# Convolution two, split over three engines, and a second paired chunk in a two-layer decoder trunk on one Trainium2 core

## The reference

```python
def odd_layer(x, g_norm, w_pw1, w_dw, b_dw, g_conv, w_pw2):
    h = rms_norm(x, g_norm)
    z = h @ w_pw1
    y = z[..., :D_MODEL] * jax.nn.sigmoid(z[..., D_MODEL:])
    y = lax.conv_general_dilated(
        y, w_dw[:, None, :].astype(y.dtype), window_strides=(1,),
        padding=[(CONV_WIDTH - 1, 0)], dimension_numbers=('NWC', 'WIO', 'NWC'),
        feature_group_count=D_MODEL) + b_dw            # CONV_WIDTH = 31, each channel by itself
    y = jax.nn.silu(rms_norm(y, g_conv))
    return x + y @ w_pw2

def channel_mixer(x, g_norm, w1, w2):
    h = rms_norm(x, g_norm)
    return x + jnp.square(jax.nn.relu(h @ w1)) @ w2
```

## Time and profile before

| | us |
|---|---|
| median of 3 runs | 2148.29 (2146.34 to 2148.51) |
| the profiled execution | 2146.37 |
| its span, first to last instruction | 2144.6 |
| TensorE busy | 2108.4 |
| GpSimd busy | 1075.8 |
| VectorE busy | 1368.5 |

### The profile page before, as it was taken

How to read it: one execution, slowest core, us unless ns; L and a number is a source line. 1 busy time by engine, 2 the same in 40 slices (tenths; PEclk the granted TensorE clock), 3 DMA queues, 4 the chain that set the end, 5 groups by cost and what they waited for, 6 DMA issues and landing times.

```text
span 2144.6 us, 30725 instructions
## 1 busy us (share of the span) xinstructions
PE 2108.4 (98%) x9946; PEld 1761.0 (82%) x9946; DVE 1368.5 (64%) x2158; ACT 876.7 (41%) x1320; POOL 1075.8 (50%) x652
## 2 busy tenths in 40 slices
PE   7999899999999999999999999999999999999999
PEld 6887788888888998888888888788888888888887
DVE  6697758888887537377777334978874324112777
ACT  6554564332332654342323342632324542323552
POOL 6865754564654004565645544746646655654000
PEclk9999999999999999999999999999999999999999
DMA  6321112323332013323333232333332333323433
GB/s 213 99 70 50 69 40 76 111 89 89 108 98 89 10 43 98 99 84 104 94 94 107 89 98 89 98 98 130 97 95 83 108 132 104 98 88 108 147 126 120
DMA packets 64128, 206.21 MB, mean 96 GB/s; under 512 B 6912, under 2 KB 7168, under 8 KB 63744
## 3 DMA queue, kind: packets, MB, share of 16 engines
q1 hardware_dynamic: 63856, 204.48, 29.9%
q10 hardware_dynamic: 144, 0.02, 0.0%
HBM read 198.18 MB, written 6.29 MB: 95 GB/s over the span
## 4 chain that ended last, share of the span: by engine, by line
PE 87%; DVE 3%; issue 2%; ACT 1%; POOL 0%; ACTq 0%; DVEq 0%; POOLq 0%
PE psum L801 24%; PE psum L803 24%; PE psum L802 24%; PE psum L976 3%; PE psum L1138 2%; PE psum L1140 2%; PE psum L1139 2%; PE psum L825 2%; PE psum L952 1%; PE psum L953 1%; DVE psum L2167 1%; PE psum L883 0%; DVE u_ring L2184 0%; PE psum L814 0%; PE psum L808 0%
## 5 line engine op out<-in xcount | busy, mean ns | idle before, releaser
L1164 POOL TENSOR_TENSOR w_buf<-raw,w_buf 128x1024 fp32r<-128x1024 f32 x302 | 735.4, 2436 | 536.4 <-ACT w_buf L1473 525.4
L801 PE MATMUL psum<-hid_buf,w_buf 128*128 128x512 f32 x1216 | 476.1, 392 | 0.0
L1473 ACT ACTIVATE w_buf<-raw 128x1024 fp32r<-128x1024 f32 x288 | 303.2, 1053 | 420.8 <-PE psum L803 385.6
L803 PE MATMUL psum<-hid_buf,w_buf 128*128 128x512 f32 x1216 | 473.5, 389 | 0.0
L802 PE MATMUL psum<-hid_buf,w_buf 128*128 128x512 f32 x1216 | 473.4, 389 | 0.0
L801 PE MATMUL psum<-h_buf,w_buf 128*128 128x512 f32 x1088 | 425.4, 391 | 1.5 <-POOL h_buf L1307 1.5
L803 PE MATMUL psum<-h_buf,w_buf 128*128 128x512 f32 x1088 | 423.4, 389 | 0.0
L802 PE MATMUL psum<-h_buf,w_buf 128*128 128x512 f32 x1088 | 423.3, 389 | 0.0
L2167 DVE SCALAR_TENSOR_TENSOR psum<-y_buf,wdw,psum 128x512 f32<-128x512 f32 x464 | 314.7, 751 | 0.0
L801 PEld LDWEIGHTS psum<-hid_buf,w_buf 128*128 128x128 f32 x1216 | 228.3, 188 | 48.0 <-issue 1.0
L802 PEld LDWEIGHTS psum<-hid_buf,w_buf 128*128 128x128 f32 x1216 | 228.4, 188 | 47.9 <-issue 1.0
(11 more groups left out here) (304 smaller groups left out, 2734.9 us busy)
## 6 DMA issues: line engine op xcount, KB each, us to landing
raw<-weights SPq DMA_DIRECT2D x334, 512.0 KB, 3.5
w_more<-weights SPq DMA_DIRECT2D x18, 512.0 KB, 4.1
xt<-x_t SPq DMA_DIRECT2D x2, 2048.0 KB, 8.4
out_t<-xt SPq DMA_DIRECT2D x16, 256.0 KB, 2.0
x_in<-x_t SPq DMA_DIRECT2D x12, 256.0 KB, 7.1
early<-weights SPq DMA_DIRECT2D x4, 512.0 KB, 7.8
x_kept<-xt SPq DMA_DIRECT2D x1, 2048.0 KB, 8.7
h_first<-x_kept SPq DMA_DIRECT2D x1, 2048.0 KB, 7.9
```

What stands on the lines that cost most here:

```text
L801: nc.tensor.matmul(acc, lhs_hi, rhs_hi, start=first, stop=False)
L803: return nc.tensor.matmul(acc, lhs_lo, rhs_hi, start=False, stop=last)
L1164: nc.gpsimd.tensor_tensor(dst_lo, src, dst_hi.bitcast(F32), ALU.subtract).then_inc(done, 1)
L1473: nc.scalar.activation(w_buf[:, 0, :, slot * P:(slot + 1) * P], raw[:, slot % 2], ACT.Copy).then_inc(hi_up, 1)
```

## The change

- `SOLO` goes from 3 to 2: chunk 2 of `ff1` leaves both halves (32 units) and becomes a second paired chunk of 56 steps, ahead of chunk 3. `ff1` half 0 now has the 32 units of chunks 0 and 1.
- Convolution two has another order and other places. Taps 1 to 30 of channel tile 0 and taps 1 to 9 of channel tile 7 (39 in all, `POOL_TAPS`) leave VectorE: ScalarE multiplies the shifted `y_buf` tile by the tap's weight into a ring of two (`scale_taps`), GpSimd adds it to `c_buf` (`add_taps`); each add waits for the one before. VectorE makes tap 0 of both tiles (`first_tap`) and taps 10 to 30 of tile 7, of which tap 10 takes the sum from `c_buf`. VectorE keeps 207 taps and the two first ones: 8 beside the last two units of the first part of pw1, 32 beside its second part, 32 beside pw2, 6 in each of the 16 slots of chunk 0, 39 in the first seven slots of chunk 1.
- GpSimd's 39 adds: 7 beside units 1 to 7 of pw1's second part, 8 beside pw2, 8 beside the up and 16 beside the down units of chunk 0.
- The squares of convolution two now follow each tile: one in slots 1 to 5 of chunk 1's up units, none in slot 6, three in slot 7.
- The loops of these places are written out on ScalarE, GpSimd and VectorE.

```diff
-SOLO = 3
+SOLO = 2
...
+ON_POOL = {0: CONV, 7: 10}
+CONV_ORDER = ([(k, ct) for group in ((0, 1, 2), (3, 4, 5), (6, 7)) for k in range(CONV) for ct in group],
+              [(k, ct) for group in ((1, 2), (3, 4), (5, 6, 7)) for k in range(CONV) for ct in group
+               if k >= ON_POOL.get(ct, 0)])
...
+POOL_TAPS = [(k, ct) for ct in ON_POOL for k in range(1, ON_POOL[ct])]
...
+PW1_TAPS = [0] * 6 + [4, 4] + [4] * 8
+PW2_TAPS = [4] * 8
+FF1_TAPS = [6] * 16
...
+PW1_POOL = [0] * 9 + [1] * 7
+PW2_POOL = [1] * 8
+FF1_POOL = [1] * 8 + [2] * 8
...
+SQUARED = (range(8), (0, 1, 2, 3, 4, 5, 6, 7))
+SQUARED_AT = ([1] * 8, [0, 1, 1, 1, 1, 1, 0, 3])
...
+            def add_taps(first, count):
+                for n in range(first, first + count):
+                    k, ct = POOL_TAPS[n]
+                    pool.wait_ge(conv_scaled, n + 1)
+                    if k == 1:
+                        pool.wait_ge(conv_first, 1 + list(ON_POOL).index(ct))
+                    if n:
+                        pool.wait_ge(conv_pool, n)
+                    T(c_buf[:, ct, :], c_buf[:, ct, :], scaled_tap(n), ALU.add).then_inc(conv_pool, 1)
...
+            def scale_taps(first, count):
+                for n in range(first, first + count):
+                    k, ct = POOL_TAPS[n]
...
+                    if n >= 2:
+                        act.wait_ge(conv_pool, n - 1)
...
+                    nc.scalar.activation(scaled_tap(n), yflat(ct, k), ACT.Copy, scale=wdw[:, ct, k:k + 1]
+                                         ).then_inc(conv_scaled, 1)
...
+                    if k and k == ON_POOL.get(ct, 0) * half:
+                        dve.wait_ge(conv_pool, POOL_TAPS.index((k - 1, ct)) + 1)
+                    total = c_buf[:, ct, :] if k and k == ON_POOL.get(ct, 0) * half else acc
```

More of the change, by code:

```diff
@@ L1294, in hidden_lo @@
                                                 flat(hidden, 0, k).bitcast(F32), ALU.subtract).then_inc(hid_lo, 1)
+                    if q == 0 and (stage, half) == ("ff1", 0):
+                        done = sum(PW1_POOL + PW2_POOL)
+                        units(first, 8, hidden_lo, taps=FF1_POOL[:8], taps_from=done)
+                        units(first + 8, 8, taps=FF1_POOL[8:], taps_from=done + sum(FF1_POOL[:8]))
+                        continue
                     units(first + 16 * q, 8, hidden_lo)
@@ L1345, in both @@
                         gate(i, r)
-                    units(first + 8, 8, both)
+                    units(first + 8, 8, both, taps=PW1_POOL[8:] if half else None)
                 else:
-                    units(first, 8)
+                    units(first, 8, taps=PW2_POOL if (name, half) == ("pw2", 0) else None, taps_from=sum(PW1_POOL))
         @block.scalar
@@ L1652, in mlp @@
                         squares = conv_squares(1)
-                    units(first + 16 * q, 8, both(hidden_hi, squares))
+                    if q == 0 and (stage, half) == ("ff1", 0):
+                        done = sum(PW1_POOL + PW2_POOL)
+                        units(first, 8, hidden_hi, taps=FF1_POOL[:8], taps_from=done)
+                        units(first + 8, 8, taps=FF1_POOL[8:], taps_from=done + sum(FF1_POOL[:8]))
+                        continue
+                    units(first + 16 * q, 8, both(hidden_hi, squares), unrolled=bool(squares))
                     job = None
@@ L1690, in _ @@
                     prepare = final(first, half, f"ff1_{half}", G_FF1, OPERAND[name, half][1])
-                    units(first, 8, both(prepare, keep_second if half else None))
+                    units(first, 8, both(prepare, keep_second if half else None), taps=None if half else PW2_POOL,
+                          taps_from=sum(PW1_POOL))
                 elif name == "pw1":
@@ L1703, in _ @@
                         act.wait_ge(conv_sum, CREDIT + 8)
-                        units(first + 8, 8, both(swish(0, h_buf), gate(1)))
+                        units(first + 8, 8, both(swish(0, h_buf), gate(1)), taps=PW1_POOL[8:])
                     else:
@@ L2261, in mlp @@
                     late = (stage, half) == ("ff1", 0)
-                    if conv and q < (SOLO - 1 if late else 3):
+                    if late and q == 0:
+                        for r in range(16):
+                            if r < 8:
+                                relu_scaled(r // 4, r % 4)
+                            else:
+                                add_residual(down, half)((r - 8) // 4, r % 4)
+                            done = FF1_FROM + sum(FF1_TAPS[:r])
+                            convolve(1, done, done + FF1_TAPS[r])
+                        continue
+                    if conv and not late and q < 3:
                         for r in range(16):
@@ L2277, in mlp @@
                         topk((5, 6), STEPS_01 + 4 * (q - 2 + 16 * q))
-                    units(up, 8, relu_scaled, more_topk(0), conv_squares(1) if late else None)
+                    if late:
+                        squares = conv_squares(1)
+                        for r in range(8):
+                            relu_scaled(r // 4, r % 4)
+                            done = FF1_FROM + sum(FF1_TAPS[:16 + r])
+                            convolve(1, done, done + FF1_TAPS[16 + r])
+                            squares(r // 4, r % 4)
+                    else:
+                        units(up, 8, relu_scaled, more_topk(0))
                     if (stage, half) == ("ff1", 1) and q == 0:
@@ L2370, in _ @@
                         link(V.memset(c_sum[:], 0.0))
-                        units(first, 8, scale_pair(0), conv_squares(0))
+                        scale, squares = scale_pair(0), conv_squares(0)
+                        for m in range(8):
+                            scale(m // 4, m % 4)
+                            squares(m // 4, m % 4)
+                            done = sum(PW1_TAPS[:m])
+                            convolve(1, done, done + PW1_TAPS[m])
                         rms_diag("conv0")
```

101 lines of the change are left out of this document (77 added, 24 removed).

## The result

| | before | after |
|---|---|---|
| median | 2147.02 (2146.34 to 2148.51) | 2158.91 (2156.95 to 2159.33) |
| profiled execution, span | 2144.6 | 2155.2 |

The ratio is 1.0052, 95% interval 1.0037 to 1.0066: slower, by 11.9 us. The forecast was 2152.6, with a range up to 2158: the time lies 6.3 us above the forecast and just outside the range. (The median of before came out 1.3 us lower this time than in the runs that the forecast was made from, so the change costs 11.9 where 4.3 was forecast; by the spans of the two profiled executions it costs 10.6.) The sign was as forecast, and both waits came from the causes that the forecast named; the sum was too small.

A forecast was written before the change was run, and what follows sets the result against it. The prediction took TensorE, busy 98% of the span, as the bound. Its terms, -21.8 + 7.5 + 17.3 + 1.3 = +4.3 us, gave a median of 2152.6 us, range 2141 to 2158.

The forecast's parts named there:

- the take-back tap: ff1 half 0, slot 12: VectorE's tap waits 16 us for GpSimd's 39 taps, making TensorE late later: +17.3 us.
- Matmuls, -21.8: Pairing chunk 2 of ff1 saves TensorE 96 matmuls at 0.2267 us each: -21.8 us.
- the unseen seam: Paired down of chunk 2 into paired up of chunk 3: inputs ready, taken as 0, bounds 0 and 2.7 us.
- GpSimd in pw1, +7.5: pw1's second part: six GpSimd adds of 1.25 us ahead of the last swish low half delay TensorE 7.5 us.
- rival C: Slower still: GpSimd's adds meet VectorE's swish products in pw1, 3 us more, pairs' seam up to 2.7; 2155.6 to 2158.3; chance 0.20.
- sign (3): ff1 half 0 trace: 16 us idle before VectorE's c_buf tap, squares' adds about 2.2 us, TensorE waits 17 us at last down part.
- Three last squares, +1.3: End of ff1 half 0's up units: three adds of squares behind the last relu make TensorE's sums wait 1.3 us.
- A: Chunk 1 of ff1 half 0: adds of squares slip between GpSimd's instructions, slot 5.14 not 6.75; 2144.5 us; chance 0.13.
- B: Slot 12 of ff1 half 0: the tap's wait isn't long, 4.6 instead of 17.3; faster, 2139.9 us; chance 0.11.

The follow-up runs named there:

- e1: Changed kernel with tile 7's nine ScalarE/GpSimd taps placed before tile 0's last fifteen, same work: 2142.55 us.
- e9: Changed kernel with only VectorE's add of squares moved behind its first tap of the next unit: 2150.87 us.
- e7: e1 with squares added earlier and the 39 GpSimd adds placed elsewhere, the last five beside chunk 1: 2127.35 us, 0.9909 of the kernel before.
- e8: e1 with squares added earlier and the five surplus GpSimd adds put into pw2, thirteen there: 2131.93 us, 0.9935 of the kernel before.
- e3: e1 with the seven GpSimd adds of pw1's second part moved to pw2 as well: 2141.08 us, 0.9971 of the kernel before.

## Why the prediction was off

Two steps failed. The sum had no term for TensorE's clock behind a wait, without a reason given: the trace shows 4.9 us. And the term of the take-back tap, right in its cause, was mis-sized: 17.3 us in the sum, 20.0 in the trace. By the forecast's own steps, against the profiled execution (10.6 us longer in its span; the forecast had 4.3):

1. **Matmuls, -21.8: right.** 96 fewer, and the second pair begins without a wait, so the unseen seam cost the 0 that was taken.
2. **GpSimd in pw1, +7.5: right** (7.1 in the trace). The page "SBUF — State Buffer" of the Trainium skill had been used for the squares only; in pw1 three of VectorE's eight swish products took over 2 us, as before the change (the earlier trace rows has one of them), so rival C's 3 us here did not come.
3. **The take-back tap, +17.3: right in kind, too small.** The low half of tile 7 at the second seam is awaited until 1583.70. On the old pace, shifted by the 8.94 us that the stage begins late, that would be 1467.75 + 87.04 + 8.94 = 1563.73: 20.0 us. The 39th tap is done when forecast (1519.8 against 1510.5 + 8.9). The 2.7 us more are: the tap itself 2.80 instead of 0.66, because it reads two SBUF operands (`y_buf` and `c_buf`) and GpSimd had begun a split at 1519.8 (+2.1); five slots of 6.5 instead of 6.75 (-1.3); a last low half 5.1 behind its relu instead of 3.8, GpSimd being busy after the short unit 22 (+1.3); and +0.6 that I did not place. I had priced the tap as a plain one, whose second operand is in PSUM. The section "Who interferes with whom" of the same page of the Trainium skill names just this form, a VectorE instruction with two SBUF inputs, and the trace agrees: 2.80 here, 0.90 in e1, where only about the last 0.3 us of a GpSimd add lay in its way. The longer tap also made the residual add of unit 13 late: the forecast had it 0.1 us behind TensorE, and unit 17 waited 2.67 us for its bank. That wait adds nothing at the seam, because VectorE comes there later still; but the 17 us were not "two or three waits" at the seam, as sign (3) had it.
4. **Three last squares, +1.3: no wait of its own.** Between the last low half and the sums lay three matmuls at the lower clock, which gave VectorE the time. The third add ended 6.4 us after its relu began and not 5.85; that it did not show was luck.
5. **The missing term: the clock, about +5.** 1.5 us behind the waits at pw2 (8 matmuls at 0.43), 0.7 before the sums and 2.7 at and behind them (the sums took 1.76 us instead of 0.95 in the earlier trace rows, nine matmuls 0.43 each). The forecast summed waits and took every matmul at 0.2267 us. The line of nines in the earlier trace rows could not have warned of it: one digit stands for some 54 us, and the page of e1 has nines throughout too, with a granted clock of 0.50 from 1571 to 1577 us. The kernel before itself falls to 0.57 and 0.51 at 252 to 256 and 259 to 262 us, in attention, under its nines. Together: 2.7 (step 3) + 4.9 (clock) - 0.4 (step 2) - 1.3 (step 4) + 0.4 (TensorE is that late already at 1330 us) = 6.3, which is 10.6 less 4.3.

Rivals A and B each left out one thing that the runs confirm is real: e9 is A as an experiment (5.15 a unit, as A had it; 8.0 us saved, A's figure), e1 is B (2142.55; B said 2139.9, without the clock). C named the right end of the range for reasons that did not hold, so that it came near the time was luck; the range itself should have had a term for a TensorE that stands.

## What to carry to other kernels

Ask of every tap, add or copy that one engine takes over from another where in the taker's list the result is fetched back, and what stands behind it in the fetching engine's list: here the order of 39 equal taps was worth 16.4 us, and the place of one add per unit another 6 to 8. Put new GpSimd work where the trace shows it idle, as e7 does in unit 8 of pw1, rather than spread evenly; two adds in a unit beside VectorE instructions with two SBUF inputs made TensorE wait 2.8 (e8) to 4.3 us (e3). When a change makes TensorE stand for several microseconds, add the slower matmuls behind the wait to its price.
